# Two causal attention jobs of a hybrid decoder layer, each run one projection group later

## What is computed

```python
h = rmsnorm(x, norm_g)
z = h @ w_in
q_a, k_a, v_a, g_a, u_p, g_p, q_m, g_m = jnp.split(z, IN_OFFSETS, axis=-1)
y_a = moba_attention(q_a, k_a, v_a) * jax.nn.silu(g_a)
y_p = multiscale_pool(u_p, w_pool, pool_scale) * jax.nn.silu(g_p)
mk, mv = jnp.split(rmsnorm(mem, mem_norm_g) @ w_mem_kv, 2, axis=-1)
y_m = memory_attention(q_m, mk, mv) * jax.nn.silu(g_m)
y = jnp.concatenate([y_a, y_p, y_m], axis=-1) @ w_out
return rmsnorm(x + y, final_norm_g)
```

## Time and profile before

| | |
|---|---|
| median of 3 runs | 436.38 us (436.27 to 436.52) |
| the profiled execution: its own time | 436.17 us |
| its span, first to last instruction | 434.0 us |
| mean granted TensorE clock | 0.997 |
| busy: TensorE | 425.5 us, 98% of the span |
| busy: VectorE, ScalarE, GpSimd | 268.2, 222.4, 27.2 us |
| HBM traffic | 89.7 MB, 207 GB/s over the span |

### The profile page before, as it was taken

How to read it: one execution, slowest core, us unless ns; L and a number is a source line. 1 busy time by engine, 2 the same in 40 slices (tenths; PEclk the granted TensorE clock), 3 DMA queues, 4 the chain that set the end, 5 groups by cost and what they waited for, 6 DMA issues and landing times.

```text
span 434.0 us, 6064 instructions
## 1 busy us (share of the span) xinstructions
PE 425.5 (98%) x2268; PEld 366.3 (84%) x2268; DVE 268.2 (62%) x293; ACT 222.4 (51%) x303; POOL 27.2 (6%) x48
## 2 busy tenths in 40 slices
PE   9999999999999999999999999999999999999993
PEld 8888888888888888888988888888899888888882
DVE  5875865364564665746466777957667574648522
ACT  6854784563534435446545545554565545357311
POOL 1000000000200000000020200001000202020200
PEclk9999999999999999999999999999999999999998
DMA  8999969898955563542626565455646496756022
GB/s 281 402 400 411 407 208 377 118 289 30 351 188 186 191 196 134 194 145 97 199 94 207 180 202 190 145 192 189 207 140 193 140 402 234 219 167 196 0 98 97
DMA packets 26522, 90.05 MB, mean 207 GB/s; under 512 B 3584, under 2 KB 4096, under 8 KB 25600
## 3 DMA queue, kind: packets, MB, share of 16 engines
q1 hardware_dynamic: 24048, 81.16, 58.2%
q10 hardware_dynamic: 2448, 8.52, 5.1%
HBM read 87.57 MB, written 2.10 MB: 207 GB/s over the span
## 4 chain that ended last, share of the span: by engine, by line
PE 96%; issue 2%; DVE 0%; POOL 0%; ACT 0%; DVEq 0%; POOLq 0%
PE ps L400 35%; PE ps L403 17%; PE ps L418 11%; PE ps L417 11%; PE ps L416 11%; PE ps L381 3%; PE ps L388 1%; PE ps L498 1%; PE ps L453 1%; PE ps L489 1%; PE ps L468 1%; PE ps L490 0%; PE ps L452 0%; PE ps L464 0%; PE ps L548 0%
## 5 line engine op out<-in xcount | busy, mean ns | idle before, releaser
L766 DVE TENSOR_TENSOR w_lo<-w_raw,w_hi 128x1024 fp32r<-128x1024 f32 x137 | 173.7, 1281 | 112.8 <-ACT w_hi L565 112.4
L565 ACT ACTIVATE w_hi<-w_raw 128x1024 fp32r<-128x1024 f32 x137 | 143.3, 1057 | 125.0 <-PE ps L403 60.6
L400 PE MATMUL ps<-xT,w_hi 128*128 128x512 f32 x640 | 201.6, 396 | 0.0
L403 PEld LDWEIGHTS ps<-xT,w_lo 128*128 128x128 f32 x640 | 120.2, 188 | 28.4
L403 PE MATMUL ps<-xT,w_lo 128*128 128x256 f32 x640 | 125.8, 278 | 0.0
L400 PEld LDWEIGHTS ps<-xT,w_hi 128*128 128x128 f32 x640 | 97.8, 189 | 0.3
L416 PE MATMUL ps<-w_hi,yT 128*128 128x512 f32 x110 | 42.8, 389 | 0.0
L417 PE MATMUL ps<-w_lo,yT 128*128 128x512 f32 x110 | 42.8, 389 | 0.0
L418 PE MATMUL ps<-w_hi,yT 128*128 128x512 f32 x110 | 42.8, 389 | 0.0
L416 PE MATMUL ps<-w_hi,xT 128*128 128x512 f32 x64 | 25.3, 396 | 0.0
L418 PE MATMUL ps<-w_hi,xT 128*128 128x512 f32 x64 | 24.9, 390 | 0.0
(11 more groups left out here) (147 smaller groups left out, 393.0 us busy)
## 6 DMA issues: line engine op xcount, KB each, us to landing
w_raw<-in_w_in SPq DMA_DIRECT2D x96, 512.0 KB, 4.3
w_raw<-in_w_out SPq DMA_DIRECT2D x32, 512.0 KB, 4.3
w_raw<-in_w_mem_kv SPq DMA_DIRECT2D x13, 512.0 KB, 13.2
x_t_raw<-in_x_t SPq DMA_DIRECT2D x8, 256.0 KB, 13.7
rows<-in_x ACTq DMA_DIRECT2D x2, 1024.0 KB, 10.0
rows<-in_mem ACTq DMA_DIRECT2D x2, 1024.0 KB, 11.8
x_res<-in_x ACTq DMA_DIRECT2D x2, 1024.0 KB, 6.4
w_raw<-in_w_mem_kv SPq DMA_DIRECT2D x5, 256.0 KB, 5.2
```

What stands on the lines that cost most here:

```text
L400: pe.matmul(ps[:, bank0(g) + f, :], hi[:, t, f * P:(f + 1) * P], moving[:, kt], start=(kt == 0), stop=(kt == KT - 1), skip_group_check=True)
L403: m = pe.matmul(ps[:, bank0(g) + f, 0:S], lo[:, t, f * P:(f + 1) * P], moving[:, kt, 0], start=False, stop=(kt == KT - 1), skip_group_chec ...
L565: act.activation(halves_of(n)[0], w_raw[:, n % RAW], ACT.Copy).then_inc(hi_done, 1)
L766: dve.tensor_tensor(lo, w_raw[:, n % RAW], hi.bitcast(F32), ALU.subtract).then_inc(lo_done, 1)
```

## The change

Job 0 moves from V1 to GA0 and job 1 from GA0 to GA1. All jobs now have their scores behind the second piece (a = 1); for the memory job that was so before. The normalisations of the causal jobs are in steps 2 and 3. The transposes stay behind piece 4 and the products with the values behind piece 6. GpSimd clears the pads in the middle of its walk over the gates, behind GA1's product, since job 1 ends later.

```diff
-CAUSAL_JOBS = {V1: 0, GA0: 1}
+CAUSAL_JOBS = {GA0: 0, GA1: 1}
 MEM_JOB = GM
-JOBS = (V1, GA0, GM)
+JOBS = (GA0, GA1, GM)
...
-BRANCHES = (V1, GA0, GP, GM)
+BRANCHES = (GA0, GA1, GP, GM)
...
-            pool.wait_ge(pv_done, 4)
-            for buf in (u_pad, sum_a, sum_b):
-                pool.memset(buf[:, :, 0:PAD], 0.0).then_inc(pads_zero, 1)
             for i, g in enumerate(GATES):
                 pool.wait_ge(gate_tanh, i + 1)
                 pool.wait_ge(att_ready, 2 * (i + 1))
                 pool.tensor_tensor(gate[:, :, :], gate[:, :, :], att[:, i % 2], ALU.mult).then_inc(gate_att, 1)
+                if g == GA1:
+                    pool.wait_ge(pv_done, 4)
+                    for buf in (u_pad, sum_a, sum_b):
+                        pool.memset(buf[:, :, 0:PAD], 0.0).then_inc(pads_zero, 1)
...
                 if g in JOBS:
-                    if a == int(g == MEM_JOB):
+                    if a == 1:
                         pe.wait_ge(evacuated, g)
                         scores(g, 0)
                         scores(g, 1)
...
                 if g in JOBS:
-                    if a == int(g == MEM_JOB):
+                    if a == 1:
                         exps(g, 0)
                         exps(g, 1)
...
                 if g in JOBS:
-                    if a == int(g == MEM_JOB):
+                    if a == 1:
                         mask_and_max(g, 0)
                         mask_and_max(g, 1)
-                if g in CAUSAL_JOBS and a in (1, 2):
-                    normalise(g, a - 1)
+                if g in CAUSAL_JOBS and a in (2, 3):
+                    normalise(g, a - 2)
```

## The result

| | before | after |
|---|---|---|
| median (lowest to highest) | 436.38 us (436.27 to 436.52, 5 runs) | 448.56 us (447.29 to 450.41, 5 runs) |
| the profiled execution | 436.17 us, span 434.0 | 450.41 us, span 448.3 |
| mean granted clock | 0.997 | 0.983 (0.983 to 0.987 over the runs) |
| waits of TensorE after its start, idle time as the view counts it | none | 9.0 us |

The ratio is 1.0277 (1.0252 to 1.0303): 12.2 us slower, where I forecast 8.8 us slower with an upper end of 447.8. The measured median lies 0.8 us outside the range. The spread is new too, 3.1 us where the kernel before has 0.25. Lines behind GpSimd's part are numbered one higher in the changed kernel (L468 is now L469, L856 L857, L766 L767), and two in TensorE's part of the filled variants (L470).

The account below looks back on a forecast made before the run. TensorE, busy 425.5 of 434.0 us and never waiting, was taken as the bound, so only new waits counted. GA0's 2.6 plus GA1's 6.3 gave 8.9 us, hence a forecast of 445.2 us, range 443.8 to 447.8.

Parts of the forecast that it names:

- no gain from leaving V1: Job 0's work leaves V1 and reappears in GA0; no wait goes with it, so the gain is 0.
- no other new wait: Evacuations, memsets, later splits, loads and the values' multiplication were all claimed to add no TensorE wait, cost 0.
- GA0, 2.6 us: In GA0 TensorE waits 0.94 us for pair 0 and 1.63 more for pair 1 before the transposes.
- GA1, 6.3 us: In GA1, beside GA0's gate work, TensorE waits 3.51 us for pair 0 and 2.76 for pair 1.
- yT's copy and low part: In GA1 ScalarE's copy (0.96 us) and VectorE's low part (1.13) stand in the chain to the transposes.
- The hand-over: From VectorE's normalisation to a waiting TensorE: taken as 0.1 us, bounds 0 and 0.2.
- By these rows it doesn't fall.: TensorE's clock stays granted through the new waits, the longest 3.5 us, so nothing is added to 8.9 us.
- The sign that I had named: Forecast would be wrong if the first matmuls behind the stall stood at twice their spacing.
- The clock as a rival: Clock falls in GA1's stall and is given back as at the start, 2.3 us lost: 447.5, chance 0.13.
- the gates' work: Rival: the gates' work in GA1 hides, so both jobs wait 2.6 us: 441.6, chance 0.06.
- the edges of a job: Rival: 0.22 us at each edge is a hidden wait that later jobs shed, 1.3 us: 435.1, chance 0.02.
- nothing runs ahead of a waiting transpose: Against the no-effect rival: TensorE runs piece 5 ahead of the waiting transposes, 436.4, chance 0.03.

Follow-up runs that it names:

- the filled variants: Changed kernel with small matmuls on constants in TensorE's waits: 39 of them (445.35 us), or about half, 2 and 4 in GA0, 8 and 6 in GA1 (445.06 us).
- The variant without waits: Changed kernel with both normalisations of each causal job in step 2, ahead of VectorE's split: 436.31 us.
- a variant with one wait of 3.9 us: Changed kernel with the normalisations still in steps 2 and 3, but each ahead of VectorE's split: 443.35 us.
- Another variant's code: Changed kernel with the causal jobs' transposes and their copies behind piece 5 instead of piece 4: median 441.78 us (439.66 to 443.60).

## Why the prediction was wrong

- **What bounds the kernel; no gain from leaving V1; no other new wait.** Right. The variant without waits takes the time of the kernel before within 0.15%.
- **GA0, 2.6 us; GA1, 6.3 us.** Right: 2.5 and 6.1 measured, the starts within 0.1 us, and confirmed by the filled variants, 445.35 and 445.06 against 445.2. The single terms held too (yT's copy and low part 2.1; a missing piece of lead 2.6 in each job). The hand-over, taken as 0.1, is 0.06: in GA1 the multiplications end at 241.29 and the transposes start at 241.35.
- **"By these rows it doesn't fall."** This step failed. I took the clock's behaviour from the tail, where it stays granted for some 5 us after the last matmul, and read this as a wait that TensorE can afford. It isn't: the clock fell in GA1, with two waits of 3.4 and 2.7 us around six transposes, in a variant with one wait of 3.9 us, and in some executions with 0.9 and 1.6 us. One tail is one sample of a thing that differs between executions of the same code. The sign that I had named came: the first matmuls behind the stalls stand at twice their spacing (1.20 us for two). The Trainium skill's rule ("TensorE: Matmul & The Clock Gate", "HAM oscillation — how this bites in real kernels") said the opposite of my row, and the trace agrees with it for GA1: the granted clock was 0.57 from 238.5 to 241.3 and 0.50 from there to 245.6.
- **The clock as a rival, 447.5 with a chance of 0.13.** The mechanism was right, its chance far too low, and its price of 2.3 us, one fall, too small: 3.2 to 3.5 us in the median, most of it in GA1 (2.4 or more), the rest put down to falls in GA0, which I hadn't counted as possible. Single falls cost 1.4 to 2.9 us in the traces. I had read the 2.3 from the start of the kernel before as 22 matmuls at 0.109 us; they are 11, each shown as two records, at 0.22, which gives the same sum by luck, and the view of stretches has the granted clock at 1.00 there, so that row doesn't show a fall. The range ended at one fall in one group.
- **The other rivals** fell: the gates' work didn't hide (6.1 us in GA1), the edges of a job are no waits to be shed (436.31 us with jobs a piece later and no wait, where 435.1 was the price), and nothing runs ahead of a waiting transpose.

No variant beats the kernel before. It has no wait to remove, so moving a job can only keep its time or lose some.

## What to carry to other kernels

When one engine is the bound, here busy for 98% of the span, a reordering is worth what it does to the slack of the side chain that feeds it. Here moving the start of a chain by one piece without moving its end cost 2.6 us a job, and placing two normalisations ahead of a split that wasn't urgent gave it all back. Put the work that TensorE waits for ahead of work that is due several pieces later. And price a TensorE wait of a few microseconds with the clock's fall on top, as a chance and for each place where it can occur; a little filler in a wait that can't be removed buys the clock back.

## What the runs showed of the hardware

- The clock fell around waits of 0.9 and 1.6 us with a burst of six transposes (0.7 us) between them, but in some executions only: one trace has 0.51 behind them, another 1.00 throughout. Another variant's code gave 439.66 us at a mean clock of 0.997 and 443.60 at 0.987. A spread of 3 us where the kernel before has 0.25 is a sign of it in the times alone.
- Filler worth about half of each wait kept the clock at 1.00 in the profiled execution and brought the spread from 3.1 to 0.5 us.
- A float32 matmul of 128 columns against a 128 x 128 tile takes 0.22 us from start to start and shows as two records (14 in 3.13 us); a float32 transpose of the same size takes some 0.11 us and shows as one (6 in 0.65). A price taken from one was wrong by half for the other.
